# One fixed expert and fifteen ranked ones, seven of them with 64 slots, and the ranking ahead of place 1

## The reference

```python
for layer in range(2):
    mod = silu(c) @ w_ada[layer] + b_ada[layer]       # six vectors: sh1, sc1, g1, sh2, sc2, g2
    u = rms_norm(h, norm_mix) * (1 + sc1) + sh1
    mix = attention and gated convolution of u        # layer 0
    mix = trailing means over 2/4/8/16 tokens, mapped # layer 1
    h = h + g1 * mix
    u = rms_norm(h, norm_ffn) * (1 + sc2) + sh2
    h = h + g2 * grouped_moe(u)
return rms_norm(h, norm_final)
```

## Time and profile before

| | us |
|---|---|
| median of 3 runs (lowest, highest) | 690.75 (689.65, 692.0) |
| the profiled execution, its time | 691.01 |
| its span, first to last instruction | 689.3 |
| PE busy | 638.2 (93%) |
| DVE busy | 354.3 (51%) |
| ACT busy | 173.2 (25%) |
| POOL busy | 97.1 (14%) |

### The profile page before, as it was taken

One profiled execution on the slowest core, in us unless ns is written; L12 is line 12 of the kernel. 1 busy time (PEld: TensorE's weight loads), 2 busy tenths in 40 slices (PEclk: granted clock), 3 DMA queues, 4 the chain that ended last, 5 costly groups with the idle time before them and its releaser, 6 DMA issues. The chain is left out here.

```text
span 689.3 us, 8320 instructions
## 1 busy us (share of the span) xinstructions
PE 638.2 (93%) x2851; PEld 331.2 (48%) x2851; DVE 354.3 (51%) x715; ACT 173.2 (25%) x436; POOL 97.1 (14%) x84
## 2 busy tenths in 40 slices
PE   5899999999899996989999999979688999999995
PEld 3455434444444452455554545468345455555441
DVE  4116699798996237843422332264686332233225
ACT  5000322333333422212121222142421121222223
POOL 0010001000000005211313321100021312213210
PEclk9999999999999998989999999989899999999998
DMA  9999998978789316999999996391769999999836
GB/s 327 360 352 379 380 322 293 373 270 285 278 310 398 149 64 212 335 391 290 351 328 372 368 336 200 95 390 56 283 229 403 330 297 365 356 369 356 273 57 245
DMA packets 68529, 203.76 MB, mean 296 GB/s; under 512 B 9614, under 2 KB 18906, under 8 KB 68485
## 3 DMA queue, kind: packets, MB, share of 16 engines
q1 hardware_dynamic: 58836, 183.63, 72.1%
q0 software_dynamic: 9040, 18.87, 11.5%
q10 hardware_dynamic: 608, 0.71, 0.3%
HBM read 189.90 MB, written 23.11 MB: 309 GB/s over the span
## 5 line engine op out<-in xcount | busy, mean ns | idle before, releaser
L1869 PE MATMUL ps<-ring,work 128*128 128x512 f32 x288 | 127.5, 594 | 0.1
L942 DVE SCALAR_TENSOR_TENSOR acc<-adaw,cond,acc 128x1024 f32<-128x1024 f32 x70 | 89.8, 1283 | 10.7 <-DMA adaw<-in_w_ada_dram 9.0
L1869 PEld LDWEIGHTS ps<-ring,work 128*128 128x128 f32 x288 | 54.1, 190 | 67.1 <-issue 66.7
L1693 PE MATMUL psY<-xu,ring 128*128 128x512 f32 x192 | 85.6, 599 | 0.0
L1394 DVE TENSOR_TENSOR work<-work,ps 128x256 f32<-128x256 f32 (+1 forms) x32 | 11.9, 372 | 128.6 <-ACT work L850 98.7
L850 ACT ACTIVATE work<-ps 128x256 f32<-128x256 f32 (+1 forms) x32 | 11.0, 344 | 227.6 <-PE ps L1869 165.6
L1908 PE MATMUL psY<-ring,work 128*128 128x512 f32 x144 | 67.2, 610 | 0.0
L1693 PEld LDWEIGHTS psY<-xu,ring 128*128 128x128 f32 x192 | 35.5, 190 | 46.1 <-issue 45.9
L610 POOL DMA_INDIRECT h_dram<-work x20 | 33.2, 1662 | 154.3 <-DVE work L1424 77.2
L843 ACT ACTIVATE work<-psA,modc,scl 128x128 f32<-128x128 f32 (+1 forms) x120 | 42.7, 436 | 43.2 <-PE psA L1846 41.5
L1424 DVE SCALAR_TENSOR_TENSOR work<-psY,work,gbc 128x512 f32<-128x512 f32 x40 | 28.2, 746 | 44.6 <-PE psY L1908 44.6
(11 more groups left out here) (260 smaller groups left out, 782.7 us busy)
## 6 DMA issues: line engine op xcount, KB each, us to landing
adaw<-in_w_ada_dram SPq DMA_DIRECT2D x84, 512.0 KB, 5.4
ring<-in_w_gate_dram SPq DMA_DIRECT2D x48, 512.0 KB
ring<-in_w_up_dram SPq DMA_DIRECT2D x48, 512.0 KB
ring<-in_w_down_dram SPq DMA_DIRECT2D x48, 512.0 KB
xu<-in_w_gate_dram SPq DMA_DIRECT2D x16, 512.0 KB
xu<-in_w_up_dram SPq DMA_DIRECT2D x16, 512.0 KB
xu<-in_w_down_dram SPq DMA_DIRECT2D x16, 512.0 KB
work<-in_w_ada_dram SPq DMA_DIRECT2D x12, 512.0 KB, 10.0
```

What stands on the lines that cost most here:

```text
L942: dve.scalar_tensor_tensor(total, adaw[:, n % ABUF, :], cond[:, k:k + 1], total if k else brow[:, :], ALU.mult, ALU.add).then_inc(mac_step, 1)
L1693: ins = pe.matmul(bank, wt, uT[:, k, :], start=(k == 0), stop=(k == KD - 1))
L1869: ins = pe.matmul(gu_ps[j % 2][:, :].rearrange("p (a f) -> p a f", a=2), xgT[:, j % 2, k, :], w_gu(j % 4)[:, :, k, :], start=(k == 0), sto ...
```

## The change

- `FIXED` is 1. Expert 0 stays in place 0, fifteen are ranked, and place 13 joins the places with 64 slots; the one-hots of places 12 and 13 become two instructions. The ranked tables grow from 14 x 14 to 15 x 15.
- SP no longer loads expert 1 ahead; place 1 is loaded after `ids`, in both layers. In layer 1 the load of expert 0 waits until all of h is reloaded.
- `sort_experts` and the first `by_place` move into `route`, between the tokens of place 0 and the one-hots of place 1. `one_hots(l, 2)` moves in front of the scaled rows of place 1.
- Table 4 moves from before the turn of place 0's hidden values to behind `turn_in` of place 2.
- `ada_total` sums in four strips of 256 columns instead of two of 512; ACT copies 256 columns and not 512.
- The last tile's logits and scores use other accumulator banks (psA for ps2), and `scores_by_token(l, 0)` stands behind `logits(l, 3)`.
- In layer 1 both halves of h are completed (`pool_in(1, 2)`, `pool_in(1, 3)`) before `turned_half(1, 1)` and `norm(3, 0)`; ACT, not DVE, writes xhat of tile 2; ACT's `norm(3, t)` order changes.
- In layer 1 PE runs three fillers once the first tile of h is complete.

```diff
-FIXED = 2
+FIXED = 1
-HALF = (5, 7, 9, 11, 14, 15)
+HALF = (5, 7, 9, 11, 13, 14, 15)
@@ SP
             load_expert(0, 0, 0)
-            load_expert(0, 1, 1, parts="ud")
...
                     sp.wait_ge(mix_banked, 2 * T)
-                    load_expert(0, 1, 1, parts="g")
-                if l == 0:
-
-                    sp.wait_ge(xg_in[1], 16)
...
                 if l == 0:
+
+                    for t in range(T):
+                        sp.wait_ge(h_in[t], 16 * 2)
                     for e in range(FIXED):
                         load_expert(1, e, e)
@@ ACT
-                for t in range(T - 1):
-                    turned_half(1, t + 1)
-                    norm(3, t)
+                turned_half(1, 1)
+                norm(3, 0)
+                norm(3, 1)
+                turned_half(1, 2)
+                norm(3, 2)
+                turned_half(1, 3)
                 norm(3, 3)
@@ DVE route
                 one_hots(l, 0)
                 tokens(l, 0)
+                link(dve.tensor_copy(cnt, ps2[:, T * E:T * E + E]))
+                if l == 0:
+
+                    mod_waits(dve, NPC - 1)
+                sort_experts(l)
+                by_place(posS, posm)
                 one_hots(l, 1)
                 tokens(l, 1)
-                dve.tensor_copy(cnt, ps2[:, T * E:T * E + E])
@@ DVE expert_loop
-                sort_experts(l)
                 xT_half(0, 0, 0)
                 room(l)
+                one_hots(l, 2)
                 xT_half(1, 1, 0)
-
-                by_place(posS, posm)
-                one_hots(l, 2)
                 one_hots(l, 3)
@@ DVE layer 1
                     turned_half(1, 0)
+                    pool_in(1, 2)
+                    pool_in(1, 3)
+                    turned_half(1, 1)
                     norm(3, 0)
-                    pool_in(1, 2)
-                    turned_half(1, 1)
-                    pool_in(1, 3)
                     turned_half(1, 2)
+                    turned_half(1, 3)
                     norm(3, 1)
-                    turned_half(1, 3)
-                    norm(3, 2)
@@ PE ada_total
-                for a in range(2):
-                    ins = pe.matmul(ps5[a * 32:(a + 1) * 32, :], ones[:, 0:32], acc[:, n % 2, a * 512:(a + 1) * 512],
-                                    start=True, stop=True)
+                for s in range(4):
+                    ins = pe.matmul(ps5[s * 32:(s + 1) * 32, 0:D // 4], ones[:, 0:32],
+                                    acc[:, n % 2, s * D // 4:(s + 1) * D // 4], start=True, stop=True)
@@ PE body
-                    if static and e == 0:
-                        token_table(l, 4)
-
...
                         turn_in(e + 2, j + 2, i + (j + 2) // 4)
+                    if e == 0:
+                        token_table(l, 4)
@@ PE layers
-                    scores_by_token(0, 0)
                 else:
+                    pe.wait_ge(back_added, 1)
+                    keep_clock(3, ps2[:, :])
...
-                    scores_by_token(1, 0)
                 logits(l, 3)
+                scores_by_token(l, 0)
                 scores_by_token(l, 1)
```

More of the change, by code:

```diff
@@ L58 @@
 RANK_AT = {p: r for r, p in enumerate([p for p in range(FIXED, E) if p not in HALF] + list(HALF))}
-HOT = [(0,), (1,), (2, 3), (4, 6), (5,), (7,), (8, 10), (9,), (11,), (12, 13), (14,), (15,)]
+HOT = [(0,), (1,), (2, 3), (4, 6), (5,), (7,), (8, 10), (9,), (11,), (12,), (13,), (14,), (15,)]
 TABLE = [(0,), (1,), (2, 3), (4, 5, 6, 7), (8, 9, 10, 11, 12, 13, 14, 15)]
@@ L64 @@
 SCATTERS = [E // 2 - sum(e % 2 == j for e in LASTS) for j in range(2)]
-HOT_BY_TABLE = [1, 2, 3, 6, 12]
+HOT_BY_TABLE = [1, 2, 3, 6, 13]
 TC, TOKC = 5, 2
@@ L71 @@
 C_ID, C_DIST, C_SLOT, C_ONE, C_TOK, C_JLT, C_FST, C_PICK, C_KEY, C_RANK, C_EID, C_HI, C_SEL, C_END = (
-    0, 128, 384, 512, 640, 648, 664, 668, 669, 683, 697, 711, 712, 728)
+    0, 128, 384, 512, 640, 648, 664, 668, 669, 684, 699, 714, 715, 731)
 POOL_MAX = 16
@@ L681, in ada_out @@
                     act.wait_ge(mod_stored[b], 16 * (n // 2))
-                act.activation(mrow[0:2 * 32, b, :], ps5[0:2 * 32, :], ACT.Copy).then_inc(row_copied, 1)
+                act.activation(mrow[:, b, 0:D // 4], ps5[:, 0:D // 4], ACT.Copy).then_inc(row_copied, 1)
                 act.wait_ge(row_copied, n + 1)
-                act.dma_start(mod_dram[l:l + 1, a * D:(a + 1) * D].rearrange("l (r n) -> (l r) n", r=2),
-                              mrow[0:2 * 32:32, b, :]).then_inc(mod_stored[b], 16)
+                act.dma_start(mod_dram[l:l + 1, a * D:(a + 1) * D].rearrange("l (r n) -> (l r) n", r=4),
+                              mrow[0:P:32, b, 0:D // 4]).then_inc(mod_stored[b], 16)
             def root_ahead():
@@ L733, in rows_out @@
                 cols = slice(T * P - P, T * P) if part else slice(0, T * P - P)
-                act.activation(logit_rows[:, cols], ps2[:, cols], ACT.Copy).then_inc(rows_copied, 1)
+                act.activation(logit_rows[:, cols], psA[:, 0:P] if part else ps2[:, cols], ACT.Copy
+                               ).then_inc(rows_copied, 1)
             def last_tile(l):
@@ L739, in last_tile @@
                 act.activation(sig_tile, sig_tile, ACT.Sigmoid).then_inc(sig_ready, 1)
-                act.activation(xhat[:, T - 1, :], h[:, T - 1, :], ACT.Copy, scale=rstd[:, T - 1:T]
-                               ).then_inc(xhat_ready, 1)
+                for t in range(T - 1 - l, T):
+                    act.activation(xhat[:, t, :], h[:, t, :], ACT.Copy, scale=rstd[:, t:t + 1]).then_inc(xhat_ready, 1)
             def spread_pool(half):
@@ L1006, in scaled @@
             def scaled(l, part):
-                if part:
-                    dve.wait_ge(std_done, (2 * l + 1) * T + T)
-                    link(dve.reciprocal(rstd[:, T - 1:T], rstd[:, T - 1:T]))
+                if part or l:
+                    t = T - 2 + part
+                    dve.wait_ge(std_done, (2 * l + 1) * T + t + 1)
+                    link(dve.reciprocal(rstd[:, t:t + 1], rstd[:, t:t + 1]))
                 dve.wait_ge(score_banked, 2 * l + part + 1)
@@ L1014, in scaled @@
                 for t in (range(T - 1, T) if part else range(T - 1)):
-                    raw = ps2[:, 0:E] if part else ps5[:, t * E:(t + 1) * E]
+                    raw = psA[:, 512:512 + E] if part else ps5[:, t * E:(t + 1) * E]
                     ins = dve.scalar_tensor_tensor(sig_tile[:, t * E:(t + 1) * E], raw, rstd[:, t:t + 1],
@@ L1174, in _ @@
             over = lasting(SORTED * SORTED, 64)
-            perm = lasting(SORTED * SORTED, 260)
+            perm = lasting(SORTED * SORTED, 292)
             picked = acc[:, 1, 0:T * SORTED * SORTED]
-            gateS = lasting(T * SORTED, 456)
-            restS = lasting(T * SORTED, 512)
+            gateS = lasting(T * SORTED, 520)
+            restS = lasting(T * SORTED, 584)
             def route(l):
@@ L1642, in logits @@
                         k = 4 * r + g
-                        ins = pe.matmul(ps2[g * 32:(g + 1) * 32, cols], wrm[:, k * E:k * E + 32], uT[:, k, cols],
+                        bank = psA[:, 0:P] if t == T - 1 else ps2[:, cols]
+                        ins = pe.matmul(bank[g * 32:(g + 1) * 32, :], wrm[:, k * E:k * E + 32], uT[:, k, cols],
                                         start=(r == 0), stop=(r == 1))
@@ L1657, in scores_by_token @@
                 for t in (range(T - 1, T) if part else range(T - 1)):
-                    dst = ps2[:, 0:E] if part else ps5[:, t * E:(t + 1) * E]
+                    dst = psA[:, 512:512 + E] if part else ps5[:, t * E:(t + 1) * E]
                     ins = pe.matmul(dst, logit_rows[:, t * P:(t + 1) * P], cst[:, C_SEL:C_SEL + E],
```

2 lines of the change are left out of this document (removed).

## The result

The changed kernel takes 696.8 us (median of 20 runs, 691.5 to 705.0) against 692.0 for the kernel before beside it (20 runs, 686.8 to 701.2): ratio 1.008 [1.006, 1.010], slower by 0.8%. The forecast was 687.2, range 683.5 to 693.0. It was wrong in size and in sign. A ratio leaves out executions over 1.5% above the fastest of their kernel: at most two of a changed kernel and five of the kernel before, but three of six in e11 and four of twelve in e13.

What follows compares the result with a forecast made beforehand. The chain of row transfers to h was taken to end each expert layer, PE to bound the first stage and pooling mixer. Terms -1.0 - 2.6 + 0.2 + 1.7 - 2.2 - 3.5 + 2.7 + 1.0 = -3.7 gave 687.2 us, range 683.5 to 693.0.

Steps and rivals of the forecast that it cites:

- Sum: +5.5 - 3.8 = +1.7 us: Layer 0, ranking ahead of place 1: first product 5.5 us later, 3.8 won back by place 2's product; range +0.2 to +3.4.
- +5.3 - 2.6 = +2.7: Layer 1, ranking ahead: first product 5.3 us later, 2.6 won back by place 2's product; range +1.2 to +4.4.
- The extra 3 MB are caught up in places 2 to 4: Experts' loop: place 1's weights, no longer preloaded, cost nothing, since PE takes 11.4 us per place there.
- The first product: Place 0's first product, behind place 1's gather (landing 5.6 us) and turn (1.1): starts at 281.8, not 276.28, in layer 0.
- gather stuck: Rival: place 1's gather must let 3 MB of weights pass, landing 6 us later per layer, 699 us; chance 0.11.
- The gain behind it, -3.8 and -2.6: From first product to place 2's product: turns fill PE's idle before table 4, less work behind it; 3.8 and 2.6 us saved.
- The rival of the slow clock: PE's clock stays at 1.2 GHz in the first product, costing 1.7 to 3.3 us more; chance 0.20.
- scores_by_token, +0.2: Layer 0's router: scores_by_token moved behind logits(3), nearly all covered by the sigmoid's table load; +0.2 us.
- Strips, -2.6: First stage, ada_total in four strips: seven sums 0.43 us shorter each, taken as -2.6 us, range -3.4 to -1.0.
- Place 13, -1.0: End of each layer, place 13 at 64 slots: only its shorter last transfer counts, -0.5 us per layer.
- Pooling and router, -5.7: Fillers before the pooling -2.2 us (range -2.6 to +0.5); new order in layer 1's router -3.5 (-4 to -1.5).
- The very end, +1.0: Output's last tile: PE idles over 6 us, the clock falls, its four rows run slower; +1.0 us (0 to +1.7).

Runs made afterwards that it cites:

- e11: Whole change without ranking ahead and fixed-expert edit, copy later, place 13 at 64 slots, plus VectorE writing layer 1's third xhat tile: ratio to before 0.986 [0.978, 0.994].
- e13: Kernel before with only place 13 run at 64 slots: ratio to before 0.995 [0.992, 0.999].
- e2: Changed kernel with VectorE's bf16 copy of the token constants moved to just before place 0's one-hots: 695.5 us, ratio to before 1.004 [1.000, 1.008].
- e9: e2 with place 1 using expert 1's weights, loaded ahead of the routing (wrong results, timing only): 694.7 us, ratio to before 1.004 [1.000, 1.007].
- e10: Kernel before with only the second fixed expert's weights no longer preloaded but issued after the ids: 697.5 us, ratio 1.005 [1.002, 1.009].
- e6: e2 with SP waiting for place 1's gathered rows before issuing the ranked experts' loads: 693.9 us, ratio to before 1.005 [1.002, 1.009].
- e12: e9 with e6's wait for place 1's rows before the ranked loads: 684.2 us, ratio to before 0.991 [0.988, 0.994].
- e1: The changed kernel again, no edit, for a second profile: 697.8 us, ratio to before 1.008 [1.005, 1.012].
- e8: e5 with the four strips of ada_total undone: 689.8 us, ratio to before 0.999 [0.996, 1.003].
- e3: Kernel before with all of the change but the fixed expert, the ranking's place, place 13 and table 4: 693.6 us, ratio 1.004 [1.001, 1.007].
- e5: e3 with VectorE's bf16 copy moved to just before place 0's one-hots: 690.8 us, ratio to before 1.0005 [0.998, 1.003].
- e15: e5 with VectorE writing layer 1's third xhat tile and xhat stored ahead of h in both layers: ratio to before 0.999 [0.996, 1.002].
- e16: e15 with the new order of stores in layer 1 alone: 686.4 us, ratio to before 0.994 [0.991, 0.997].

## Why the prediction was wrong

*The step that failed: "Sum: +5.5 - 3.8 = +1.7 us", and in layer 1 "+5.3 - 2.6 = +2.7".* The route from tokens to reload was put at +1.2 and +2.2 us; it came out at +5.8 and +7.9 (e2: +5.7 and +5.9). Both terms of the sum failed. The first product starts 8.7 and 7.9 us later and not 5.5 and 5.3, and of the -3.8 and -2.6 behind it there came -1.8 and +1.3.

*The step "The extra 3 MB are caught up in places 2 to 4"* is not what made this kernel slow. PE waits nowhere for weights in it, P2 to reload is 1.2 and 1.3 us shorter than before, and e9, without the 3 MB, is no faster than e2. But the step is wrong, and only the late first product hides it: where the first product is not late or less so, in e10 and e6, P2 to reload grows by 3.7 and 1.8 us over before and by 3.8 and 4.0 over e2. Rows 1 had the warning, and I read it aloud: PE busy throughout and DMA at 1.02. I then treated them as one bound at a time. e6, e9 and e12 show that each of the two takes over where the other is removed.

*The first product.* VectorE's part was right (ids +2.75 us, tokens of place 1 +6.3). The landing of place 1's gather was set at 5.6 us from a range of 4.6 to 8, and measured 8.3 and 7.7: with e6's 4.1 beside it, the collision with the weights is shown. The turn behind it takes 1.8 us to the first product and not 1.1. The rival "gather stuck" named the place, and its price (6 us more) was over twice too high: 2.1 to 2.7 over my value. The Trainium skill (DMA: Bandwidth & Descriptors, Queues, rings and completion order), which has the engines take turns between queues, would have the gather slowed and not stuck. The trace does not decide it. The gather is issued 3.3 us after the first load of place 1, so at the 352 GB/s of rows 1 some 2 MB were still ahead of it, an estimate; to let them pass would take 5.7 us on top of the 4.1, at most 9.8, and it landed in 8.3.

*The gain behind it, -3.8 and -2.6.* P0 to P2 was put at 24.1 us in both layers and is 26.2 and 28.0, in e2 28.0 and 26.2, and in e12, with neither cost, still 26.5 and 26.6. PE's wait before table 4 shrank from 2.95 to 1.91, but table 4 still comes 19.3 and 20.2 us after P0 (before 18.9 and 19.1). Its one-hots on VectorE (304.22 to 309.05) stand behind table 3, which PE computes between the first products, and the first of these ran partly at the lower clock: 5.28 and 6.11 us for ten instructions, before 4.46 and 4.56. The down product behind table 4 was put at 3.5 us, its time at full clock. It takes 5.38 and 6.33, and in layer 0 of the kernel before it had taken 5.29, a row that the prediction did not read:

```profile
299.08 5.29 PE L1908 MATMUL psY<-ring,work 128*128 128x512 f32 x8
```

The rival of the slow clock is thus a part of it, after PE's waits of 4.13 and 5.39 us, though it priced the first product alone; the clock is the last number but two of the window:

```profile
284.00:292.00 8.00, 3.99 (x12) 2.74 (x13) 3.78 (x12) 2.20 (x6) 0.00 (x0) 0.57 0.99 379
```

*The copy's stall.* No step had it: "scores_by_token, +0.2" priced PE's move and not what it does to VectorE's place beside POOL. The last scores and the copy come 0.8 us later against the memset, and a 0.25 us copy takes 5.0: +4.4 in the profile. e2 against e1 is 0.4% with overlapping intervals, so that all executions stall is not shown. The Trainium skill (SBUF — State Buffer, Who interferes with whom) says that a copy or a cast on VectorE can take the port pair that it shares with GpSimd, under a lock for a whole instruction that goes to the one that issues first. The trace agrees in kind: the copy ends at 265.70, the memset at 265.58. It does not agree in the order, since the copy's record starts 1.35 us ahead of the memset's. That the ports are the cause is not shown; e2 shows that the copy takes 0.26 us once the memset is over.

*Strips, -2.6.* The group of the ten sums in the kernel after, from 30 to 257 us:

```profile
L1548 PE MATMUL ps<-acc,cst 128*32 128x256 f32 x80 | 7.3, 438 | 2.1 <-DVE acc L944 2.1
```

The eight at full clock take 0.64 us each ((7.3 - 1.08 - 1.06) / 8), near the estimate. Little of it arrived: PE waits 2.12 us for VectorE where it waited 1.3 and runs that sum at half the clock, and e8 finds no difference. PE's busy row was taken for the bound of the stage. That the stage follows VectorE, which waits 15.8 us there for the weights of ada, is argued and not shown.

*Place 13, -1.0.* Right mechanism, wrong size: the shorter last transfer gives 1.4 us per layer where I took 0.5. POOL issues it 6.8 us after its rows are ready, where the prediction had said 3 us or more.

*Pooling and router, -5.7.* Right: -5.9 (e2: -7.1). But in e3 and e5 alone it does not arrive, because the tokens now come sooner after the last stores (3.3 us after SP issued them in e5, 5.2 before), and the gather waits for the stores; e15 and e16 show it.

*The very end, +1.0.* Right: +1.3, with PE idle 5.76 us and four rows at 3.78.

So 10.3 us of the 17.7 between 687.3 and the profiled 705.0 come from the two routes, 4.4 from the copy, 2.8 from stage 1. In e2, without the stall and near the median, 8.2 of 9.6 come from the routes and 2.3 from stage 1, and pooling and router give 1.4 back.

## What to carry to other kernels

Where two resources are full in the same stretch, price every edit on both, and test by removing both costs at once: one alone will seem to be worth nothing. Moving an instruction that orders nothing still moves what it runs beside; look up what each neighbour engine does within some us of it. When a stage is shortened, look at what used its length: here the stores of the tile that the next stage reads first should go ahead of those needed later.

## What was not expected of the hardware

A VectorE copy of 128 elements to bf16 stood 5.0 to 5.5 us beside a GpSimd memset of 3.53 us, and this went with where it started: 2.15 us ahead of the memset's record it took 0.25 (three profiles), at 1.89 us ahead 5.54, at 1.35 to 1.37 ahead 5.0 (three profiles). The same gather of one place took 4.1 us from its issue to the turn with no weights beside it (e6), 8.3 beside their stream.
